# An encoder block on one core: the first norm's token factor moved from before the input product to behind it

## The reference, cut to what matters

```python
def rms_norm(x, g):
    y = xf * lax.rsqrt(jnp.mean(xf * xf, axis=-1, keepdims=True) + RMS_EPS)
    return (y * g)
...
h = concatenate([meta, x])                      # 16 + 256 = 272 tokens, 2048 features
hn = rms_norm(h, norm1_g)
q, k, v, u, g_na, g_ssm = split(hn @ w_in)      # 1024 each, the two gates 2048 each
y_na = neighbourhood_attention(q, k, v, na_rpb) @ w_proj_na
y_ssm = s5_branch(u, ...) @ w_proj_ssm          # a two-way scan over the tokens, in 64 groups
mixed = sigmoid(g_na) * y_na + sigmoid(g_ssm) * y_ssm
h = h + mixed @ w_out
h = h + conv_gated_ffn(rms_norm(h, norm2_g), ...)
```

## Time and profile before

| | |
|---|---|
| median of 3 runs | 1667.15 us |
| the profiled execution's own time | 1664.67 us |
| its span, first to last instruction | 1662.9 us |
| mean granted TensorE clock | 0.974 of full |
| PE, POOL, ACT, DVE busy | 95%, 73%, 49%, 34% of the span |
| HBM read and written | 259 MB and 9.5 MB |

### The profile page before, as it was taken

The page is one execution under the profiler, slowest core; times in us unless marked ns, Lnnn a source line. Parts: engine busy times, 40 slices in busy tenths (PEclk is TensorE's granted clock), DMA queues, the critical chain, the costliest instruction groups (busy, mean ns, idle before and its releaser), DMA issues.

```text
span 1662.9 us, 35955 instructions
## 1 busy us (share of the span) xinstructions
PE 1573.5 (95%) x12943; PEld 1525.3 (92%) x12943; DVE 562.7 (34%) x1149; ACT 808.7 (49%) x1351; POOL 1217.3 (73%) x682
## 2 busy tenths in 40 slices
PE   5589799999998999999999999999999999999996
PEld 3589799999987888899999999999999999999996
DVE  3108377874984333134232122222222222000002
ACT  3386334444775444644444554555555554333333
POOL 2575775879653656578877888888888887888883
PEclk9699899999998999999999999999999999999999
DMA  6553543665113554455654565655565656555552
GB/s 189 99 169 120 146 131 110 195 183 151 54 38 102 152 151 141 129 164 188 233 176 153 179 187 181 185 179 182 181 188 178 184 181 201 191 192 194 194 190 101
DMA packets 252906, 267.82 MB, mean 161 GB/s; under 512 B 38108, under 2 KB 240380, under 8 KB 252204
## 3 DMA queue, kind: packets, MB, share of 16 engines
q1 hardware_dynamic: 220496, 251.69, 48.5%
q10 hardware_dynamic: 32284, 15.27, 3.6%
q0 software_dynamic: 64, 0.07, 0.0%
HBM read 259.33 MB, written 9.52 MB: 162 GB/s over the span
## 4 chain that ended last, share of the span: by engine, by line
PE 82%; POOL 7%; issue 4%; ACT 3%; DVE 1%; DMA 1%; SPq 1%; POOLq 1%; ACTq 0%; DVEq 0%
PE ps L1365 19%; PE ps L1367 18%; PE ps L1366 18%; POOL w_lo L407 6%; PE ps L1676 5%; PE ps L1677 5%; PE ps L1678 5%; PE ps L1531 2%; PE ps L1473 2%; PE ps L1567 1%; PE ps L1465 1%; PE ps L1510 1%; PE ps L1393 1%; PE ps L1518 1%; PE ps L1588 1%
## 5 line engine op out<-in xcount | busy, mean ns | idle before, releaser
L407 POOL TENSOR_TENSOR w_lo<-w_raw,w_hi 128x1024 fp32r<-128x1024 f32 x440 | 1056.6, 2412 | 331.3 <-ACT w_hi L403 330.3
L403 ACT ACTIVATE w_hi<-w_raw 128x1024 fp32r<-128x1024 f32 x464 | 489.3, 1059 | 647.7 <-PE ps L1367 450.4
L1365 PE MATMUL ps<-act_hi,w_hi 128*128 128x258 f32 (+2 forms) x2432 | 706.7, 291 | 43.4 <-POOL w_lo L407 22.5
L1367 PE MATMUL ps<-act_hi,w_lo 128*128 128x258 f32 (+2 forms) x2432 | 697.3, 287 | 0.0
L1366 PE MATMUL ps<-act_lo,w_hi 128*128 128x258 f32 (+2 forms) x2432 | 696.1, 286 | 0.0
L1365 PEld LDWEIGHTS ps<-act_hi,w_hi 128*128 128x128 f32 x2432 | 468.6, 193 | 60.6 <-issue 25.8
L1366 PEld LDWEIGHTS ps<-act_lo,w_hi 128*128 128x128 f32 x2432 | 469.4, 193 | 0.0
L1367 PEld LDWEIGHTS ps<-act_hi,w_lo 128*128 128x128 f32 x2432 | 467.2, 192 | 0.0
L1676 PE MATMUL ps<-hidden_hi,w_hi 128*128 (+1 forms) x704 | 194.5, 276 | 2.2 <-DVE gelu_ring L1318 2.2
L1678 PE MATMUL ps<-hidden_hi,w_lo 128*128 (+1 forms) x704 | 194.5, 276 | 0.0
L1677 PE MATMUL ps<-hidden_lo,w_hi 128*128 (+1 forms) x704 | 194.4, 276 | 0.0
(11 more groups left out here) (241 smaller groups left out, 2070.4 us busy)
## 6 DMA issues: line engine op xcount, KB each, us to landing
w_raw<-in_w_up SPq DMA_DIRECT2D x176, 512.0 KB, 3.5
w_raw<-in_w_in SPq DMA_DIRECT2D x128, 512.0 KB, 3.8
w_raw<-in_w_down SPq DMA_DIRECT2D x88, 512.0 KB, 3.7
w_raw<-in_w_out SPq DMA_DIRECT2D x32, 512.0 KB, 3.4
w_raw<-in_w_proj_na SPq DMA_DIRECT2D x16, 512.0 KB, 3.4
w_raw<-in_w_proj_ssm SPq DMA_DIRECT2D x16, 512.0 KB, 3.4
w_raw<-in_w_glu SPq DMA_DIRECT2D x8, 512.0 KB, 3.4
bias_ring<-skew_scratch ACTq DMA_DIRECT2D x32, 96.0 KB, 2.7
```

The costliest lines, as they stand in the source:

```text
L403: act.activation(slot(whi, k), slot(raw, k), ACT.Copy).then_inc(s_hi, 1)
L407: pool.tensor_tensor(slot(wlo, k), slot(raw, k), slot(whi, k).bitcast(F), ALU.subtract).then_inc(s_lo, 1)
L1365: mm(o, slot(whi, k)[:, cols], xh[:, kt, lo:lo + n], start=kt == 0, stop=False)
L1367: ins = mm(o, slot(wlo, k)[:, cols], xh[:, kt, lo:lo + n], start=False, stop=kt == units * UKT - 1)
```

## The change

The input product now runs on x·g. ACT makes its high part straight from `x0T` with the weight g as scale, DVE its low part from PSUM (`x_lo`), and POOL's and PE's parts of the first norm are gone. PE's program mixes the transposes with the first four units. r comes from the tokens as loaded: ACT squares them with a sum (6 instructions), DVE and ACT make r per token (`tst`), DVE spreads it on diagonals (`dg`), PE sends these through ones to get `rstd`. r is then applied where results leave PSUM:

- u: DVE instead of ACT writes the 128 pieces, times r;
- k and q: DVE scales the two banks in place (`scale_block`), and ACT's `store_block` waits for that (`s_sc`) instead of for `s_used`;
- v: ACT's copies behind the transposes take the token's factor as scale; one of them is split in two;
- gates: DVE instead of ACT copies them out, times r.

The scan's 67 steps are cut into portions of 9, with a scale or a gate between them. ACT issues 8 of the parameter DMAs before its first work and the 8 of `b_raw` and `c_rows` one behind each of units 4 to 11's `w_hi`. POOL clears `Wn` earlier, in another place.

```diff
 # ACT
+for k in range(KT):
+    act.wait_ge(s_xt, k + 1)
+    act.activation(hnh[:, k, :], x0T[:, k, :], ACT.Copy, scale=gains[:, k:k + 1]).then_inc(s_nh, 1)
+    if k % 4 == 1:
+        hi_unit(act, 0, k // 4)
+for t, n in ((0, P), (1, P), (2, N_META)):
+    for h in range(2):
+        act.activation(sqj[0:n, :], xtok[0:n, t, h * HALF:(h + 1) * HALF], ACT.Square,
+                       accum_out=tst[0:n, t, h:h + 1]).then_inc(s_tsq, 1)
+        act.wait_ge(s_tsq, 2 * t + h + 1)
+act.wait_ge(s_var, 1)
+act.activation(tst[:, :, 2], tst[:, :, 2], ACT.Sqrt).then_inc(s_sd, 1)
+for k in range(8):
+    hi_unit(act, U_U + DEPTH, k)
+    act.dma_start(dst, src).then_inc(s_par, 16)     # loads[k]: b_raw x4, c_rows x4
...
 # ACT, in k_blocks, behind the block's last hi_unit
-                        act.wait_ge(s_used, 8 * i + (U_K + k + 1))
+                        act.wait_ge(s_sc, 2 * i + (k // 4 + 1))
...
 # DVE
+def x_lo(k):
+    dve.wait_ge(s_nh, k + 1)
+    dve.scalar_tensor_tensor(out=hnl[:, k, :], in0=ps[:, 4 + k % 3, 0:L], scalar=gains[:, k:k + 1],
+                             in1=hnh[:, k, :].bitcast(F), op0=ALU.mult, op1=ALU.subtract).then_inc(s_nl, 1)
+def scale_block(banks, lo, done):
+    two = ps[:, banks:banks + 2, 0:n]
+    dve.tensor_tensor(two, two, rstd[:, lo:L].unsqueeze(1).to_broadcast([P, 2, n]), ALU.mult).then_inc(done, 1)
...
+for i in range(PAIRS // 8):
+    in_block(i, i == PAIRS // 8 - 1)
+    dve.wait_ge(s_used, U_K + 4 * (i + 1))
+    scale_block(2 * (i % 2), 0, s_sc)
...
+for n in range(4 + G_SCAN):
+    for c in range(min(SCAN_STEPS * n, NCH - 1), min(SCAN_STEPS * (n + 1), NCH - 1)):
+        scan_step(c)
...
+    if n < 4:
+        dve.wait_ge(s_used, U_Q + 4 * (n + 1))
+        scale_block(2 * (n % 2), LIVE, s_sc)
+    else:
+        dve.wait_ge(s_used, U_G + 4 * (n - 3))
+        gate_block(gate_na, 2 * (n - 4), 2 * (n % 2))
...
 # DVE, at the end of out_block
+                dve.wait_ge(s_used, U_G + 4 * G_SCAN + 4 * (i + 1))
+                gate_block(gate_na, 2 * i + 2 * G_SCAN, 0)
...
 # PE
+for k in range(4):
+    x_transposes(k)
+for q in range(4):
+    for m in range(2):
+        if q < 3:
+            x_transposes(4 * q + 4 + 2 * m)
+            x_transposes(4 * q + 5 + 2 * m)
+        pe.wait_ge(s_nl, UKT * (q + 1) + SEED)
+        half_unit(U_U, q, q, 4, m, hnh, hnl, 0, L, m)
+pe.wait_ge(s_dg, 1)
```

More of the change, by code:

```diff
@@ L488, in _ @@
             pool.drain()
-            for k in range(DEPTH - 1):
+            for k in range(DEPTH):
                 lo_unit(pool, 0, k)
-            norm_lo(pool, 0, L)
-            lo_unit(pool, 0, DEPTH - 1)
             pool.dma_start(pad_d, padt[:, 0:PADW]).then_inc(s_pad1, 16)
@@ L626, in _ @@
[L626 to L639 removed]
+                    loads.append((cnat[:, d, :, r, :], c[0, d].rearrange("(k g) c n -> (g c) k n", k=KH)))
@@ L642, in _ @@
+            for k in range(8):
+                hi_unit(act, U_U + DEPTH, k)
+                dst, src = loads[k]
+                act.dma_start(dst, src).then_inc(s_par, 16)
+            with act.Fori(1, ITERS_IN) as i:
+                for k in range(8):
+                    hi_unit(act, (U_U + DEPTH) + 8 * i, k)
             v = lambda n: prm[:, n, :]
```

244 lines of the change are left out of this document (116 added, 128 removed).

## The result

The changed kernel takes 1681.6 us, the median of 5 runs (1679.7 to 1682.8), against 1667.15 for the kernel before beside it. The ratio estimated from the runs is 1.0062, with a 95% interval of 1.0039 to 1.0085 (the two medians divided give 1.0087). It is slower by 0.6%, and lies 6 us above the stated range. Its profiled execution took 1680.07 us with a span of 1678.3. One execution of all that follow, of `y_gates_first`, took 2201 us at a granted clock of 0.65, and its median and ratio leave it out.

What follows compares the result with a forecast made beforehand. PE, busy 95% of the span, was taken as the bound, so only its waits and slowed clock count. 26.7 - 16.5 - 5.4 - 4.0 - 1.2 = -0.4 us gave 1666, range 1653 to 1676.

Steps and rivals of the forecast that it cites:

- The end of the U product: Input product at the start: ends at 88.5 us, 27.7 earlier than before.
- The fourth unit: Start of the U product: transposes and four weight units end on PE at 38 us, from a first unit at 16.5.
- The pause ahead of the fifth unit: U product: PE pauses 9 us while r is made, plus 1.8 for the lowered clock.
- rival 3: U product: DMA issues stretched by weights and spill starve it, ending at about 97; 8.5 us more, 1675; chance 0.16.
- The gain up to K: From the start to K's first transpose: 26.7 us gained (16 to 30).
- U to K: Between U product and K's first transpose: DVE's u pieces delay the parameter chain; 1 us lost (0 to 4).
- The K block ends: K product: DVE's scale delays ACT's store and `wt_copy`; three pauses of 3.7 us plus 1.8 for the clock, 16.5 lost.
- Q and the gates: Ahead of the gates: PE waits for the late fourth Q scale, a pause of 5.6 us; 5.4 lost with the clock.
- The failed step of the sum: Gates: DVE's copies are done in time beside PE's next block, so no loss was counted.
- The y product: PE waits for DVE's gate copies: 4.0 us lost in the middle, about 1.2 at the end.
- The failed step of the base: Starting time: profiled execution 1664.7 us, 2.5 below the median; second norm and all behind it taken as unchanged.

Runs made afterwards that it cites:

- y_gates_first: Changed kernel with DVE's three late gate copies placed earlier (sixth gate block between two `g_fwd`, y product's ahead of the last two `y_copy`): 1677.7 us.
- combined_meta: combined_spill with DVE's second pair of `g_nat` moved behind the sixth gate block's copy and the subtraction ACT's exponential waits for: 1646.5 us, ratio to before 0.9843.
- squares_spill: Changed kernel with ACT's squares between its tile copies and units 5 to 7 loaded ahead of the spill: 1684.1 us, one profiled execution.
- combined_spill: Changed kernel with earlier K scales and y gate copies, 8 scan steps, squares between tiles, units 5 to 7 loaded before the spill: 1646.9 us, ratio 0.9838.

## Why the prediction was wrong

- **The end of the U product** was right, 88.8 for 88.5, in part by luck. The fourth unit ended at 38.8 for 38, of parts that were off: PE began its first unit at 17.9 for 16.5 and ran half of it at half clock, which the sum doesn't have. Against that, the transposes were cheaper than the sum has them: the 0.83 us per tile from the earlier trace rows, called full clock in the prediction, is from the time ahead of the first record of the clock too, and at full clock two tiles take 1.0 us (26.86 to 27.86 in the changed kernel). The pause ahead of the fifth unit was 7.6 us (4.85 + 2.71) for 9, with two more holders than r, SP's weights behind the spill and POOL's transfer, that the prediction did not see. The issues were stretched as rival 3 had it, all eight from 15.1 us to 22.3, but behind the fifth unit PE waited only 1.07 us (at 63.56): with units prepared ahead, ACT caught up. The Trainium skill's page "DMA: Bandwidth & Descriptors" says in the section "Issuing engines are not separate DMA queues" that the sequencer's time to initiate a DMA is usually small relative to the DMA itself. For these short rows the traces disagree: in the kernel before, the eight issues took 15.1 of the 19.1 us until the last of the loads had landed, and in the changed kernel three of the four `b_raw` issues took 4.0 to 5.4 us of ACT. (The section "Anatomy of one DMA", which the prediction named too, calls the generation of descriptors small, but describes DMAs issued by GpSimd; these are issued by ACT.) The gain up to K was 24.5 for 26.7; U to K cost 2.9, not 1.
- **The K block ends** were right: three pauses of 3.14 to 3.21 for 3.7, and 14.9 us for 16.5 when they were taken away. The chain was the one described.
- **Q and the gates** were right in kind: 5.30 us for 5.6 of pause, and a lead of 5.4 us behind the first gate unit for 4.8.
- **The failed step of the sum** is "During the gates DVE is done in time; its copy lies beside PE's next block." That holds for five of the six blocks. The sixth has no next block: PE needs its banks for `k_meta` at once, and in DVE's program its copy stands behind two `g_fwd`. PE waited 6.25 us instead of 1.73. This is 4.5 us where the sum has 0. (From the gates' begin to `k_meta` the changed kernel took 78.3 us and the kernel before 72.2; some 1.9 of these 6.1 are the half clock behind the wait ahead of the gates, which the sum had.) Undone in `combined_meta`, it gives back 4.6 (213.0 to 208.4). The order of DVE's instructions shows it as plainly as at the K blocks; the prediction followed it there and not here.
- **The y product** cost 4.5 for 4.0 in the middle and 2.2 for 1.2 at the end.
- By these the changed kernel is 5.2 us behind at 529.84, 2.7 behind at 1409.53 (the 3.4 us at half clock near 710 us that before had are missing, and 1.7 us of the 2.5 with them), where the forecast said 0.4. By the later profiles it is about 10 and 3 to 9.
- **The failed step of the base** is "The profiled execution took 1664.7, 2.5 below the median of the runs shown", and with it the assumption that all behind the second norm is the same in both. In time this step weighs most. The profile of before had its down product in a pace that two other profiles of it don't have. The median of three runs carried part of the same luck: with more runs beside each experiment the kernel before had medians of 1671.7 to 1673.8. The pace at the new address is a term that the sum doesn't have: 1.9 us. From the forecast of 1667.5 by the median to 1681.6 it is 14.1 us: some 5 are the base (1672.5), 4.5 the sixth block, 1.9 the pace, and 2.7 are not assigned; the stages up to 530 us differ by more than that between profiles of one kernel.
- The measured +0.6% is thus made of 5 to 10 us of waits, of which 2 to 4 come back before 1400 us, where the changed kernel has fewer stretches of half clock, of a pace 0.02 us per unit slower, and of a base that was drawn low beside it; against the later medians of before the same 1681.6 us is 0.5% slower. What is shown by undoing it: the K ends (16 us by the medians), Q to gates (7.7), the sixth block (4.6 by the trace), the weights behind the spill (3.4 by the trace). What is only read from rows: POOL's transfer as the last holder of the fifth unit once the weights are early.

## What to carry to other kernels

When a step that releases a bank moves to another engine, write down for every block, the last one above all, what stands ahead of it in that engine's program and what waits for it behind. The placement decided here, not the amount of work: the same 0.7 us multiply cost 5 us at each block end behind the last copy and nothing ahead of it, and put right, the change gives 1.5 to 1.7% instead of taking 0.6%. And before a sum is made against one profiled execution, see by a second profile of the same program that its untouched stages take the same time.

## What the runs showed of the hardware

- Back-to-back matmuls of 256 columns at full clock, with nothing waited for, keep one pace through a stage of 240 us. It differed between executions of one program (units of 24 in 2.720 us once and in 2.826 twice) and with the placement of the tiles (2.826, 2.848 and 2.880). Why is open. The up product, of 258 columns, stayed at 2.87 in all 20 traces. Per column that is 0.464 ns for 2.874, 0.460 to 0.469 for the three common paces of 256 columns, and 0.443 for the rare 2.720.
- One issue of a short-row DMA on ACT (`b_raw`, 256 KB) took from 0.4 to 8.15 us: the first of the four 0.4 in each of the 20 traces, the others 1.9 to 5.6. The 8.15 stands in three traces (`squares_spill`, `combined_spill`, `combined_meta`), each time beside the spill of 2176 KB.
- POOL's transfer of 56 KB (`rpb_pad`), issued 0.8 us behind the spill on another queue, landed 0.2 to 0.3 us behind it in all 14 traces of the changed kernel and its variants (43.75 behind 43.54 in the changed kernel). In the kernel before, with the spill long over, it took 4.7 us. A small transfer didn't pass a large one there.
- In the first units of the changed kernel, from 17.9 us on, matmuls of 272 columns began 0.226 us apart and later 0.126 apart, while the windows there show a granted clock of 1.00. The trace has no record of the clock ahead of 21.75 us, and the spacing changes 0.4 us behind that record. In the kernel before, the sums of squares (272 columns, in fp32) begin 0.455 us apart up to its first record at 26.9 and 0.23 behind it. A granted clock of 1.00 ahead of a trace's first record says nothing.
- Beside POOL's `w_lo` three of DVE's products of 128 x 160 took 2.5 us each (four took 7.92), about as long as POOL's subtraction of 2.4. Four of them took 1.83 in the kernel before, beside POOL's products of the same shape.
